# A depthwise convolution on TensorE: fp32r products with a fold, and fp32 products of 32 output columns

## The chip, the cores and the metric

The kernel runs on one core of one Trainium2 chip. Its engines are TensorE (matmul; PE in the profile, PEld its weight loads), VectorE (DVE), ScalarE (ACT), GpSimd (POOL) and SyncE (SP, which issues most DMAs). The metric is the device time of one execution in microseconds; lower is better.

## The reference, cut to what matters

A trunk of two layers handles 336 tokens (16 meta tokens, 256 prompt tokens, 8 samples of 8 tokens). Each layer mixes tokens in two ways from one projection `u = rmsnorm(h) @ w_in`: pooling windows over 512 channels, and a convolution module over 512 others. Then come a projection `w_out` and a channel mixer, dense in layer 0, eight experts in layer 1.

```python
def _conv_module(a_past, z, dw_w, dw_b, ln_g, ln_b, pw_w):      # CONV_KERNEL = 31 taps
    v = z[..., :CONV_WIDTH] * jax.nn.sigmoid(z[..., CONV_WIDTH:])
    ext = jnp.concatenate([a_past.astype(v.dtype), v], axis=1)
    y = lax.conv_general_dilated(ext, dw_w[:, None, :], window_strides=(1,), padding='VALID',
        dimension_numbers=('NWC', 'WIO', 'NWC'), feature_group_count=CONV_WIDTH) + dw_b
    y = jax.nn.silu(_layernorm(y, ln_g, ln_b))
    return y @ pw_w, ext[:, ext.shape[1] - CONV_BUF:]
```

The convolution is depthwise: each of the 512 channels has its own 31 taps. The change touches the 272 tokens of meta and prompt; the 64 sample tokens are convolved on VectorE before and after.

## The kernel before, in words

Channels lie on partitions, tokens along the free dimension; the 512 channels make four tiles, c = 0 to 3, of 128. Weights stream through a ring of six buffers (`raw`); ScalarE rounds each slot to fp32r (`w_hi`), VectorE makes the rest (`w_lo`), both in rings of three, and a product is three fp32r matmuls (`mm3`: hi·hi, hi·lo, lo·hi; lines 1747 to 1749). PSUM has six banks for products in turn: every group of products waits for the evacuation of the group six earlier (`evac`, counted in one fixed order, `GROUP`).

The projection `w_in` is worked in six slots of 256 columns in the order 2, 4, 3, 5, 1, 0 (`w_in_slot(0)` to `w_in_slot(4)`, then the last by hand): values and gates of channel tiles 0 and 1, values and gates of tiles 2 and 3, then the pooling channels. When both halves of a gate are there, VectorE forms v (`gated`, after a tanh on ScalarE) into `conv_ext`. SP then writes a tile to DRAM (`shifted`) and reads it back in another layout (`x_turned`): partition 32 i + j holds channel j of a group g of 32 channels, shifted by some tokens that depend on i. So one matmul with 128 rows takes four taps of 32 channels at once.

Before the change a tile goes this way:

1. `tap_blocks` (VectorE, L1312): stationary blocks of 128 x 128 from the taps, in a hi and a lo part, into the buffers `w_hi` and `w_lo` that the weight slots use too.
2. `turned_high` (ScalarE, L931) and `turned_low` (VectorE, L1320): hi and lo of `x_turned`, 1168 columns.
3. `conv_parts` (TensorE): for each of the four groups g, two shifts of three fp32r matmuls of 276 columns into a bank. The output partitions 32 q + j are partial sums that belong q tokens apart.
4. `part_rows` (ScalarE, L948): copies of 32 partitions and two banks, each quarter q shifted by q tokens, into `raw`; one `evac` for two banks.
5. `conv_fold` (TensorE, L1927): four fp32 matmuls with a stationary of ones (`spread_blk`) add the quarters up into one bank; `conv_with_bias` (ScalarE) moves it to `y`.

TensorE's order is `w_in_slot(2)`, half of slot 3, `conv_parts(0)`, the other half, `conv_parts(1)`, `conv_fold(0)`, `w_in_slot(4)`, `conv_fold(1)`, `conv_parts(2)`, `conv_parts(3)`, both last folds, and then the layer norm: the mean (L1906), half of the last `w_in` slot with the sums of squares inside (L1962), and the spread of the factor (L1779), after which the pointwise product can follow. VectorE's order is written out by hand as well; `conv_samples` (L1256, L1258), the tokens of the samples, fills it between the steps. GpSimd's pooling windows (L708 to L718) start with `pool_in(4, 0)` on VectorE.

Of the kernel before, what the change touches and what calls it, by code (L numbers as in the profile page):

```python
# [15 lines left out]
P = 128  # L16
MM_BANKS = 6
RAW = 6
SPLIT = 3
# [4 lines left out]
def hybrid_trunk(nc, x_prompt, x_sample, state_pool, state_conv, meta_tokens, norm1_g, w_in, pool_w,  # L24
# [35 lines left out]
    SHIFTS = 2  # L60
    NX = TP + NB
    XW = CSEG + 2
    XN = NX + NB * NB * (SHIFTS - 1)
    TAPW = NB * NB * SHIFTS
    ZERO = P - BLK
    O_COLS = NB * TP
# [39 lines left out]
    def plan_parts(l, c):  # L106
        if len(GROUP) % 2:
            plan(("even", l, c))
        plan(*[("part", l, c, g) for g in range(NB)])

    plan(*[("x", k) for k in range(KD // 2)], ("params",), *[("x", k) for k in range(KD // 2, KD)])
    for l in range(L):
# [3 lines left out]
        plan(("win", l, 2 * WIN_ORDER[3]))  # L116
        plan_parts(l, 0)
        plan(("win", l, 2 * WIN_ORDER[3] + 1))
        plan_parts(l, 1)
        plan(("conv", l, 0), *[("win", l, 2 * WIN_ORDER[4] + i) for i in (0, 1)], ("conv", l, 1))  # L120
        plan_parts(l, 2)
        plan_parts(l, 3)
        plan(("conv", l, 2), ("conv", l, 3))
# [20 lines left out]
    with ExitStack() as ctx:  # L144
# [15 lines left out]
        spread_blk = wide[:, 0:ZERO + P]  # L160
        one_blk = wide[:, ZERO:ZERO + BLK]
# [21 lines left out]
        tap_hi = sb("tap_hi", [P, L * KC, TAPW], F32R, dense)  # L183
        tap_lo = sb("tap_lo", [P, L * KC, TAPW], F32, dense)
# [9 lines left out]
        y_pool = sb("y_pool", [P, NG, T], F32, mixer)  # L194
        m_all = sb("m_all", [P, 2, KD, T], F32R, mixer)
# [7 lines left out]

        m_flat = m_all[:].rearrange("p i k t -> p (i k t)")
        turned = m_flat[:, 0:4 * NB * XN].rearrange("p (b h g n) -> p b h g n", b=2, h=2, g=NB)

# [74 lines left out]
        TAP_BLOCKS = ps[:, 7, P:P + NB * L * KC * 2 * NB].rearrange("p (g o n) -> p g o n", g=NB, o=L * KC)  # L281
# [17 lines left out]
        e_hi_done, e_lo_done, y_ready = sem("e_hi_done"), sem("e_lo_done"), sem("y_ready")  # L299
        tap_hi_done, tap_lo_done, taps_spread = sem("tap_hi_done"), sem("tap_lo_done"), sem("taps_spread")  # L300
        blocks_done, factors_done = sem("blocks_done"), sem("factors_done")
        part_out = sem("part_out")
        e_sent = [sem(f"e_sent{i}") for i in (0, 1)]
        e_turned = [sem(f"e_turned{i}") for i in (0, 1)]
# [126 lines left out]
        def parts_out(l, c):  # L431
            return tile_raw(l, c)[:, 0:O_COLS].rearrange("p (g t) -> p g t", g=NB)

# [8 lines left out]
        def dense_used():  # L442
            out, n_w = [], 0
            for n in range(MOE_BASE):
# [8 lines left out]
                elif b == FFN_BASE:  # L453
                    u, i = divmod(n - b, 2)
                    out.append((mm_done, GROUP[("gu", u, 2 * i + 1)] + 1))
                else:
                    l, i = MIX_BASE.index(b), n - b
                    last = (("win", l, 2 * WIN_ORDER[W_AT.index(i)] + 1) if i in W_AT else
                            ("part", l, D_AT.index(i), NB - 1) if i in D_AT else
                            ("pool", l, POOL_ORDER[-1]) if i == S_POOL_W else  # L460
                            ("pw", l, KC - 1) if i == S_PW else ("wout", l, 2 * (i - S_OUT) + 1))
                    out.append((mm_done, GROUP[last] + 1))
# [16 lines left out]
        def wait_used_dense(eng, n):  # L479
            s, v = DENSE_USED[n]  # L480
            eng.wait_ge(s, v)
# [55 lines left out]
        def _(sp):  # L537
# [8 lines left out]
            def turn_tiles(l, half):  # L546
# [6 lines left out]
                for c in tiles:  # L553
# [87 lines left out]
        def _(pool):  # L641
# [15 lines left out]
            link(nc.gpsimd.memset(spread_blk, 0.0))  # L657
# [205 lines left out]
        def _(act):  # L863
# [18 lines left out]
            def mixer_layer(l):  # L882
# [43 lines left out]
                def turned_high(c):  # L926

                    act.wait_ge(e_turned[c % 2], 16 * NB * (2 * l + c // 2 + 1))
                    if c > 1:
                        act.wait_ge(mm_done, GROUP[("part", l, c - 2, NB - 1)] + 1)  # L930
                    nc.scalar.activation(turned[:, c % 2, 0], x_turned(l, c), ACT.Copy).then_inc(e_hi_done, 1)  # L931

# [5 lines left out]
                def part_rows(c, pairs=(0, 2)):  # L938

                    if pairs[0] == 0 and ("even", l, c) in GROUP:  # L940
                        act.wait_ge(evac, GROUP[("even", l, c)])
                        act.sem_inc(evac, 1)
                    for g in pairs:
                        at = GROUP[("part", l, c, g)]
                        act.wait_ge(mm_done, at + 2)
                        for q in range(NB):
                            rows = slice(BLK * q, BLK * (q + 1))
                            nc.scalar.activation(parts_out(l, c)[rows, g:g + 2, :],  # L948
                                                 ps[rows, at % MM_BANKS:at % MM_BANKS + 2, q:q + TP], ACT.Copy
                                                 ).then_inc(part_out, 1)  # L950
                        act.wait_ge(part_out, 2 * NB * (KC * l + c) + NB * (g // 2 + 1))
                        act.wait_ge(evac, at)
                        act.sem_inc(evac, 2)

                past_rows()
                gated(0)
                if l == 0:
                    act.wait_ge(taps_spread, 1)
                    nc.scalar.activation(tap_hi[:].rearrange("p o (g n) -> p g o n", g=NB), TAP_BLOCKS, ACT.Copy
                                         ).then_inc(tap_hi_done, 1)  # L960
# [12 lines left out]
                part_rows(3)  # L973
                conv_with_bias(2)
# [6 lines left out]
                split_to(b + W_AT[5])  # L981
                conv_with_bias(3)
# [182 lines left out]
        def _(dve):  # L1165
# [79 lines left out]
            def mixer_layer(l):  # L1245
# [30 lines left out]
                def value(half):  # L1276
                    for i in (0, 1):
# [25 lines left out]
                def tap_blocks(c):  # L1303

                    if l == 0 and c == 0:
                        dve.wait_ge(tap_lo_done, 1)
                        dve.wait_ge(consts, 2)
                    n = b + D_AT[c]
                    _, hi, lo = parts(n, slot_size(n))
                    wait_used_dense(dve, n - SPLIT)  # L1310
                    for out, taps in ((hi, tap_hi[:, KC * l + c, :].bitcast(F32)), (lo, tap_lo[:, KC * l + c, :])):
                        nc.vector.tensor_tensor(out.rearrange("p (k n) -> p k n", k=TAPW),  # L1312
                                                one_blk.unsqueeze(1).broadcast_to([P, TAPW, BLK]),
                                                taps.unsqueeze(2).broadcast_to([P, TAPW, BLK]), ALU.mult
                                                ).then_inc(blocks_done, 1)

                def turned_low(c):

                    dve.wait_ge(e_hi_done, KC * l + c + 1)
                    nc.vector.tensor_tensor(turned[:, c % 2, 1], x_turned(l, c), turned[:, c % 2, 0].bitcast(F32),  # L1320
                                            ALU.subtract).then_inc(e_lo_done, 1)
# [15 lines left out]
                if l == 0:  # L1337
                    dve.wait_ge(tap_hi_done, 1)
                    nc.vector.tensor_tensor(tap_lo[:].rearrange("p o (g n) -> p g o n", g=NB), TAP_BLOCKS,
                                            tap_hi[:].bitcast(F32).rearrange("p o (g n) -> p g o n", g=NB), ALU.subtract  # L1340
                                            ).then_inc(tap_lo_done, 1)
# [392 lines left out]
        def _(pe):  # L1734
# [98 lines left out]
            def mixer_layer(l):  # L1833
# [56 lines left out]
                if l == 0:  # L1890

                    pe.wait_ge(consts, 2)
                    for g in range(NB):
                        for i in range(NB):
                            taps = tap_rows.rearrange("p o (m j) -> p o m j", m=SHIFTS)[:, :, :, NB * i:NB * (i + 1)]
                            ins = nc.tensor.matmul(TAP_BLOCKS[:, g].rearrange("p o (m q) -> p o m q", m=SHIFTS),
# [11 lines left out]
                def conv_parts(c):  # L1908

                    hi, lo = dense_slot(b + D_AT[c], P)  # L1910
                    pe.wait_ge(blocks_done, 2 * (KC * l + c + 1))
                    pe.wait_ge(e_lo_done, KC * l + c + 1)
                    for g in range(NB):
                        out = group(("part", l, c, g))
# [311 lines left out]
```

## Time and profile before

| | before |
|---|---|
| median of 3 runs | 1523.79 us (1523.72 to 1525.31) |
| the profiled execution | 1527.42 us |
| its span, first to last instruction | 1525.6 us |
| PE, DVE, ACT busy | 1477.9, 1203.8, 964.3 us |
| experts' stage | 547 to 1506 us of the span |

Times below are microseconds from the start of the profiled span unless marked ns. Busy time of an engine counts overlapping instructions once. A matmul of fp32 operands shows as two records, each with its weight load; one of fp32r operands as one.

### The profile page before, as it was taken

What the parts mean: (1) busy time and instruction counts of PE and PEld (TensorE: products, weight loads), DVE (VectorE), ACT (ScalarE), POOL (GpSimd) and SP (SyncE); (2) the same over time, 40 slices, a digit from 0 to 9 for tenths busy, and PEclk for the clock granted to TensorE, in tenths of its full rate; (3) what the DMA queues carried; (4) which work ended last, traced back from release to release, by engine and by line L of the source; (5) the groups of instructions that cost most, each with busy time, mean ns of one, the idle gap of its engine ahead of it and who ended that gap; (6) DMA issues with size and microseconds to landing.
All of it is one profiled execution on the core that took longest, in us unless ns stands there. A gap on an engine that the chain in (4) does not pass through costs nothing.

```text
span 1525.6 us, 20888 instructions
## 1 busy us (share of the span) xinstructions
PE 1477.9 (97%) x7639; PEld 1288.8 (84%) x7639; DVE 1203.8 (79%) x1001; ACT 964.3 (63%) x812; POOL 185.0 (12%) x216
## 2 busy tenths in 40 slices
PE   8989999999988999999999999999999999999995
PEld 7979999999987987888888888888888888888884
DVE  4887755544488578988888888888888888888888
ACT  4574334333256377777777777777777777777773
POOL 1156100002124106910000000000000000000002
PEclk9999999999998999999999999999999999999998
DMA  6455998344055569999999999999999999999994
GB/s 198 114 194 157 313 301 241 97 155 143 31 139 167 168 211 391 395 379 396 377 388 367 378 386 370 373 390 366 385 387 358 387 385 360 389 381 370 384 380 137
DMA packets 249678, 453.40 MB, mean 297 GB/s; under 512 B 9605, under 2 KB 99781, under 8 KB 249631
## 3 DMA queue, kind: packets, MB, share of 16 engines
q1 hardware_dynamic: 245056, 442.20, 81.5%
q0 software_dynamic: 2960, 9.73, 2.1%
q10 hardware_dynamic: 1615, 0.85, 0.2%
q8 instruction: 28, 0.46, 0.1%
q14 instruction: 19, 0.16, 0.0%
HBM read 426.38 MB, written 26.37 MB: 297 GB/s over the span
## 4 chain that ended last, share of the span: by engine, by line
issue 55%; PE 6%; POOL 4%; DMA 2%; DVE 1%; ACT 1%; POOLq 0%; DVEq 0%; ACTq 0%
PE ps L1747 1%; PE ps L1748 1%; PE ps L1749 1%; POOL xg L775 1%; POOL h L799 1%; DMA xg<-og,row_i 1%; DMA og<-obuf,out_row_i 0%; DMA h<-last_row 0%; DMA last_row<-last_pos 0%; POOL key L787 0%; PE ps L2104 0%; POOL pick L795 0%; POOL og L808 0%; DVE w_lo L531 0%; PE ps L2002 0%
## 5 line engine op out<-in xcount | busy, mean ns | idle before, releaser
L531 DVE TENSOR_TENSOR w_lo<-raw,w_hi 128x2048 fp32r<-128x2048 f32 x336 | 764.5, 2290 | 117.5 <-ACT w_hi L526 116.3
L526 ACT ACTIVATE w_hi<-raw 128x2048 fp32r<-128x2048 f32 x334 | 639.5, 1916 | 123.7 <-PE ps L1749 122.2
L1749 PE MATMUL ps<-w_hi,xg_lo 128*128 128x512 f32 x896 | 351.4, 392 | 0.0
L1748 PE MATMUL ps<-w_lo,xg_hi 128*128 128x512 f32 x896 | 350.8, 391 | 0.0
L1747 PE MATMUL ps<-w_hi,xg_hi 128*128 128x512 f32 x896 | 350.8, 391 | 0.0
L1748 PEld LDWEIGHTS ps<-w_lo,xg_hi 128*128 128x128 f32 x896 | 168.3, 188 | 37.2
L1747 PEld LDWEIGHTS ps<-w_hi,xg_hi 128*128 128x128 f32 x896 | 168.3, 188 | 36.8 <-DVE w_lo L531 0.2
L1749 PEld LDWEIGHTS ps<-w_hi,xg_lo 128*128 128x128 f32 x896 | 168.3, 188 | 36.0
L1747 PE MATMUL ps<-x_hi,w_hi 128*128 128x336 f32 x580 | 187.8, 324 | 8.1 <-DVE x_lo L1412 3.2
L1748 PE MATMUL ps<-x_lo,w_hi 128*128 128x336 f32 x580 | 184.9, 319 | 0.0
L1749 PE MATMUL ps<-x_hi,w_lo 128*128 128x336 f32 x580 | 184.1, 317 | 0.0
L1747 PE MATMUL ps<-w_hi,ft_hi 128*128 128x512 f32 x448 | 180.4, 403 | 0.3 <-DVE w_lo L531 0.3
L1749 PE MATMUL ps<-w_hi,ft_lo 128*128 128x512 f32 x448 | 176.0, 393 | 0.0
L1748 PE MATMUL ps<-w_lo,ft_hi 128*128 128x512 f32 x448 | 175.4, 392 | 0.0
L511 DVE TENSOR_TENSOR w_lo<-raw,w_hi 128x2048 fp32r<-128x2048 f32 (+3 forms) x39 | 80.2, 2062 | 55.5 <-ACT w_hi L502 54.1
L1747 PEld LDWEIGHTS ps<-x_hi,w_hi 128*128 128x128 f32 x580 | 110.1, 190 | 12.1 <-issue 5.7
L808 POOL DMA_INDIRECT og<-obuf,out_row_i x6 | 10.3, 1712 | 830.3 <-SPq L633 828.7
L502 ACT ACTIVATE w_hi<-raw 128x2048 fp32r<-128x2048 f32 (+3 forms) x41 | 70.3, 1721 | 63.5 <-PE ps L1749 62.2
L1748 PEld LDWEIGHTS ps<-x_lo,w_hi 128*128 128x128 f32 x580 | 110.1, 190 | 0.4
L1749 PEld LDWEIGHTS ps<-x_hi,w_lo 128*128 128x128 f32 x580 | 109.8, 189 | 0.0
L1749 PEld LDWEIGHTS ps<-w_hi,ft_lo 128*128 128x128 f32 x448 | 84.1, 188 | 18.6
L1747 PEld LDWEIGHTS ps<-w_hi,ft_hi 128*128 128x128 f32 x448 | 84.2, 188 | 17.4 <-DVE w_lo L531 1.2
(288 smaller groups left out, 1711.5 us busy)
## 6 DMA issues: line engine op xcount, KB each, us to landing
raw<-in_moe_w_gate_dram SPq DMA_DIRECT2D x112, 1024.0 KB, 7.4
raw<-in_moe_w_up_dram SPq DMA_DIRECT2D x112, 1024.0 KB, 7.6
raw<-in_moe_w_down_dram SPq DMA_DIRECT2D x112, 1024.0 KB, 7.5
raw<-in_w_in_dram SPq DMA_DIRECT2D x11, 1024.0 KB, 5.1
raw<-in_ffn_w_gate_dram SPq DMA_DIRECT2D x11, 1024.0 KB, 6.0
raw<-in_ffn_w_up_dram SPq DMA_DIRECT2D x11, 1024.0 KB, 6.3
raw<-in_w_out_dram SPq DMA_DIRECT2D x8, 1024.0 KB, 5.5
obuf<-ones SPq DMA_DIRECT2D x15, 512.0 KB, 8.0
```

The source lines that it names most:

```text
L502: nc.scalar.activation(hi, r, ACT.Copy).then_inc(hi_done, 1)
L511: nc.vector.tensor_tensor(lo, r, hi.bitcast(F32), ALU.subtract).then_inc(lo_done, 1)
L526: nc.scalar.activation(hi, r, ACT.Copy).then_inc(hi_done, 1)
L531: nc.vector.tensor_tensor(lo, r, hi.bitcast(F32), ALU.subtract).then_inc(lo_done, 1)
L775: nc.gpsimd.indirect_dma_start(out=xg, out_offset=bass.IndirectOffsetOnAxis(ap=row_i[:, t, k:k + 1], axis=0), in_=hs[:, t, :], in_offset=N ...
L799: link(nc.gpsimd.tensor_tensor(pick_e[:, i, NE * c:NE * (c + 1)], pick[:, i, NE * c:NE * (c + 1)], iota_e[:], ALU.mult))
L808: nc.gpsimd.indirect_dma_start(out=og[:, i, t, :], out_offset=None, in_=obuf, in_offset=bass.IndirectOffsetOnAxis(ap=out_row_i[:, i, t:t + ...
L1747: nc.tensor.matmul(out, a_hi, b_hi, start=start, stop=False)
L1748: nc.tensor.matmul(out, a_hi, b_lo, start=False, stop=False)
L1749: return nc.tensor.matmul(out, a_lo, b_hi, start=False, stop=stop)
```

## The change

A tile is now convolved with 32 fp32 matmuls: for each of eight steps r and each group g, a stationary of 128 rows and 32 columns, placed at columns 32 g of the array, so that its output is the partitions 32 g to 32 g + 31 of one bank. The four taps 4 r to 4 r + 3 lie in the 128 rows, and all eight steps add up in PSUM. So the fold, the copies of partial sums, `turned` and the hi and lo of taps and blocks go; the stationary blocks (`blocks`) are fp32 of their own, in memory that `m_all` takes later. `x_turned` is read back with shifts of one token and not four, 300 columns and not 292. The diag slots no longer write `w_hi` and `w_lo`, and the wait of a later split goes back to the slot before them. The order on TensorE, VectorE and ScalarE changes with it. Core of the diff:

```diff
+    STEPS = 8
-    XN = NX + NB * NB * (SHIFTS - 1)
-    TAPW = NB * NB * SHIFTS
+    XN = TP + NB * (STEPS - 1)
+    TAPW = NB * STEPS
...
+        plan(*[("win", l, 2 * WIN_ORDER[3] + i) for i in (0, 1)], ("conv", l, 0), ("conv", l, 1))
+        plan(*[("win", l, 2 * WIN_ORDER[4] + i) for i in (0, 1)], ("conv", l, 2), ("conv", l, 3))
...
+        blocks = sb("blocks", [P, KC, TAPW, BLK], F32, diag)
...
         def wait_used_dense(eng, n):
+            while n >= 0 and is_diag(n):
+                n -= SPLIT
+            if n < 0:
+                return
...
-                        src = shifted[KC * l + c].rearrange("(g c) n -> c g n", g=NB)[:, :, NB * i:NB * i + XN]
-                        sp.dma_start(x_turned(l, c)[BLK * i:BLK * (i + 1)], src).then_inc(e_turned[c % 2], 16)
+                        src = shifted[KC * l + c].rearrange("(g c) n -> c g n", g=NB)[:, :, i:i + XN]
+                        sp.dma_start(x_turned(l, c)[BLK * i:BLK * (i + 1)], src).then_inc(e_turned[c], 16)
...
         @block.scalar
...
-                turned_high(0)
-                turned_high(1)
-                part_rows(0, (0,))
                 split_to(b + W_AT[4])
-                part_rows(0, (2,))
                 gated(1)
-                part_rows(1)
                 conv_with_bias(0)
-                turned_high(2)
-                turned_high(3)
                 conv_with_bias(1)
-                part_rows(2)
-                part_rows(3)
-                conv_with_bias(2)
...
                 split_to(b + W_AT[5])
+                conv_with_bias(2)
                 conv_with_bias(3)
...
         @block.vector
...
                 split_to(b + W_AT[3])
                 tap_blocks(0)
-                value(1)
-                turned_low(0)
                 tap_blocks(1)
-                turned_low(1)
-                gate(1, (0,))
-                conv_samples(0)
-                dve.wait_ge(evac, GROUP[("part", l, 0, NB - 1)] + 1)
-                gate(1, (1,))
+                value(1, (0,))
+                conv_samples(0, (0,))
+                value(1, (1,))
+                conv_samples(0, (1,))
+                gate(1)
                 gated(1)
                 split_to(b + W_AT[4])
                 tap_blocks(2)
                 tap_blocks(3)
-                dve.wait_ge(evac, GROUP[("conv", l, 0)] + 1)
+                conv_samples(1)
+                dve.wait_ge(evac, GROUP[("conv", l, 1)] + 1)
                 pool_in(4, 0)
-                split_to(b + D_AT[3])
-                conv_samples(1, (0,))
-                turned_low(2)
-                turned_low(3)
                 pool_in(4, 1)
-                conv_samples(1, (1,))
                 conv_samples(2)
                 conv_samples(3)
...
         @block.tensor
...
+                def conv_tile(c):
+                    out = group(("conv", l, c))
+                    pe.wait_ge(blocks_done, KC * l + c + 1)
+                    pe.wait_ge(e_turned[c], 16 * NB * (l + 1))
+                    for r in range(STEPS):
+                        for g in range(NB):
+                            ins = nc.tensor.matmul(out[BLK * g:BLK * (g + 1), 0:TP], blocks[:, c, STEPS * g + r, :],
+                                                   x_turned(l, c)[:, g, NB * r:NB * r + TP], start=r == 0,
+                                                   stop=r == STEPS - 1, tile_position=(0, BLK * g))
                     ins.then_inc(mm_done, 1)
...
+                w_in_slot(3)
+                conv_tile(0)
+                conv_tile(1)
+                w_in_slot(4)
+                conv_tile(2)
+                conv_tile(3)
```

## Rows read from the trace of the kernel before

**Rows 1.** The page: the span and TensorE's share of it.

```profile
span 1525.6 us, 20888 instructions
PE 1477.9 (97%) x7639; PEld 1288.8 (84%) x7639; DVE 1203.8 (79%) x1001; ACT 964.3 (63%) x812; POOL 185.0 (12%) x216
```

**Rows 2.** Windows: stretch, length, busy time of each engine, clock, DMA share, GB/s.

```profile
52.70:97.00 44.30, 36.70 (x215) 32.44 (x214) 39.84 (x43) 31.05 (x46) 17.14 (x15) 0.96 0.50 148
...
547.00:1506.00 959.00, 957.21 (x4324) 785.26 (x4324) 841.91 (x492) 719.39 (x491) 75.35 (x59) 1.00 1.01 373
```

**Rows 3.** Timeline of PE, layer 0: start, length, instruction, [idle before <- releaser].

```profile
41.55 0.40 PE L1747 MATMUL ps<-x_hi,w_hi 128*128 128x336 f32 x1
...
52.71 0.29 PE L1747 MATMUL ps<-m_all,w_hi 128*128 128x276 f32 x1
53.09 0.28 PE L1747 MATMUL ps<-m_all,w_hi 128*128 128x276 f32 x1
...
62.69 0.40 PE L1747 MATMUL ps<-m_all,w_hi 128*128 128x276 f32 x1 [1.54 <-ACTq L953]
...
67.00 0.42 PE L1747 MATMUL ps<-x_hi,w_hi 128*128 128x336 f32 x1 [0.70 <-DVE w_lo L511]
67.57 0.31 PE L1747 MATMUL ps<-x_hi,w_hi 128*128 128x336 f32 x1
68.03 0.32 PE L1747 MATMUL ps<-x_hi,w_hi 128*128 128x336 f32 x1
...
74.50 1.99 PE L1927 MATMUL ps<-raw,wide 128*128 128x272 f32 x8
...
90.51 3.55 PE L1927 MATMUL ps<-raw,wide 128*128 128x272 f32 x8 [3.30 <-ACTq L953]
93.85 2.67 PE L1906 MATMUL ps<-y,ones 128*128 128x336 f32 x8
99.15 2.43 PE L1962 MATMUL ps<-ones,z 128*112 128x1 f32 x24
104.89 0.80 PE L1779 MATMUL ps<-scratch,ones 112*128 112x336 f32 x2
```

**Rows 4.** The same timeline in layer 1: slot 2's first record, and the spread.

```profile
414.71 0.39 PE L1747 MATMUL ps<-x_hi,w_hi 128*128 128x336 f32 x1
...
484.20 0.73 PE L1779 MATMUL ps<-scratch,ones 112*128 112x336 f32 x2
```

**Rows 5.** Lines by source: count, ns least/median/most, first and last start.

```profile
L1962 PE MATMUL ps<-ones,z x48: 165/237/237, 99.1 to 479.2; 128*112 128x1 f32 x48
L1927 PE MATMUL ps<-raw,wide x64: 390/392/793, 64.3 to 470.4; 128*128 128x272 f32 x64
L948 ACT ACTIVATE raw<-ps x64: 613/616/622, 55.3 to 466.2; 32x544 f32<-32x544 f32 x64
L1312 DVE TENSOR_TENSOR w_hi<-wide,tap_hi x8: 1217/1220/1222, 44.9 to 445.7; 128x1024 fp32r<-128x1024 f32 x8
```

**Rows 6.** Timeline of ACT, layer 0: the first use of a tile read back.

```profile
48.34 1.18 ACT L931 ACTIVATE m_all<-raw 128x1168 fp32r<-128x1168 f32 x1 [6.17 <-DMA raw<-shifted]
```

**Rows 7.** Timeline of POOL, layer 0: first and last of 12 rows, windows of two groups.

```profile
72.19 1.94 POOL L708 TENSOR_TENSOR win_sum<-pool_ext 128x470 f32<-128x470 f32 x1 [42.85 <-DVE pool_ext L1328]
...
90.26 0.31 POOL L718 TENSOR_TENSOR y_pool<-win_sum,pool_ext 128x64 f32<-128x64 f32 x1
```

**Rows 8.** Timeline of DVE, layer 0: sample taps, gate, first v, last split, last factor.

```profile
41.30 0.44 DVE L1296 SCALAR_TENSOR_TENSOR conv_ext<-z 128x272 f32<-128x272 f32 x1 [2.19 <-ACT z L923]
...
55.23 1.19 DVE L1256 TENSOR_TENSOR scratch<-conv_ext,params 128x992 f32<-128x992 f32 x1 [0.24 <-DVE z L1288]
...
62.66 0.51 DVE L1288 TENSOR_TENSOR z<-ps,rstd 128x336 f32<-128x336 f32 x1 [2.28 <-ACTq L953]
...
64.66 2.29 DVE L511 TENSOR_TENSOR w_lo<-raw,w_hi 128x2048 fp32r<-128x2048 f32 x1 [0.18 <-DVEq L508]
...
104.23 0.51 DVE L1209 TENSOR_TENSOR scratch<-ident,nt 112x336 f32<-112x336 f32 x1
```

More of the change, by code:

```diff
@@ L298, in hybrid_trunk @@
         m_hi_done = sem("m_hi_done")
-        e_hi_done, e_lo_done, y_ready = sem("e_hi_done"), sem("e_lo_done"), sem("y_ready")
-        tap_hi_done, tap_lo_done, taps_spread = sem("tap_hi_done"), sem("tap_lo_done"), sem("taps_spread")
+        y_ready = sem("y_ready")
+        tap_cols_done, taps_spread = sem("tap_cols_done"), sem("taps_spread")
         blocks_done, factors_done = sem("blocks_done"), sem("factors_done")
-        part_out = sem("part_out")
         e_sent = [sem(f"e_sent{i}") for i in (0, 1)]
-        e_turned = [sem(f"e_turned{i}") for i in (0, 1)]
+        e_turned = [sem(f"e_turned{c}") for c in range(KC)]
         ln_centred, ln_sq = sem("ln_centred"), sem("ln_sq")
@@ L458, in dense_used @@
                     last = (("win", l, 2 * WIN_ORDER[W_AT.index(i)] + 1) if i in W_AT else
-                            ("part", l, D_AT.index(i), NB - 1) if i in D_AT else
+                            ("conv", l, D_AT.index(i)) if i in D_AT else
                             ("pool", l, POOL_ORDER[-1]) if i == S_POOL_W else
@@ L924, in gated @@
                                              ).then_inc(tanh_done, 1)
[L926 to L931, printed above, removed]
                 def pooled_high(g):
@@ L936, in pooled_high @@
                     nc.scalar.activation(pooled_at(g)[0], y_pool[:, g, :], ACT.Copy).then_inc(pooled_hi, 1)
[L938 to L953, printed above, removed]
                 past_rows()
@@ L1275, in mixer_layer, with value @@
                 dve.sem_inc(sums_read, 1)
-                def value(half):
-                    for i in (0, 1):
+                def value(half, outs=(0, 1)):
+                    for i in outs:
                         g = ("win", l, 2 * WIN_ORDER[2 * half] + i)
@@ L1305, in tap_blocks @@
                     if l == 0 and c == 0:
-                        dve.wait_ge(tap_lo_done, 1)
+                        dve.wait_ge(tap_cols_done, 1)
                         dve.wait_ge(consts, 2)
[L1308 to L1321, printed above, removed]
+                    nc.vector.tensor_tensor(blocks[:, c], one_blk.unsqueeze(1).broadcast_to([P, TAPW, BLK]),
+                                            tap_cols[:, KC * l + c, :].unsqueeze(2).broadcast_to([P, TAPW, BLK]),
+                                            ALU.mult).then_inc(blocks_done, 1)
                 def pool_in(s, i):
@@ L1906, in mean_of @@
                     return nc.tensor.matmul(SUM_BANK, ones[:], y[:, c, :], start=(c == 0), stop=(c == KC - 1))
[L1908 to L1914, printed above, removed]
-                        for m in range(SHIFTS):
-                            at = NB * NB * m
-                            ins = mm3(out[:, 0:NX], hi[:, SHIFTS * g + m, :], lo[:, SHIFTS * g + m, :],
-                                      turned[:, c % 2, 0, g, at:at + NX], turned[:, c % 2, 1, g, at:at + NX],
-                                      m == 0, m == SHIFTS - 1)
-                        ins.then_inc(mm_done, 2 if g == 0 and ("even", l, c) in GROUP else 1)
@@ L1922, in conv_fold @@
-                def conv_fold(c):
-                    out = group(("conv", l, c))
-                    pe.wait_ge(evac, GROUP[("part", l, c, NB - 1)] + 1)
-                    for g in range(NB):
-                        ins = nc.tensor.matmul(out[:, 0:TP], spread_blk[:, ZERO - BLK * g:ZERO + P - BLK * g],
-                                               parts_out(l, c)[:, g, :], start=g == 0, stop=g == NB - 1)
-                    ins.then_inc(mm_done, 1)
-                w_in_slot(3, (0,))
-                conv_parts(0)
```

54 lines of the change are left out of this document (10 added, 44 removed).

## The prediction

> **What bounds the kernel now.** First I read the page: TensorE is busy for 97% of the span [rows 1]. That alone says little, so next come the windows by stage. In the experts' stage, 959 of the 1526 us, PE is busy for 957 at full clock [rows 2]. Nothing of that stage changes, and it starts only after the routing, which needs the whole mixer of layer 1. So what the mixers win or lose reaches the end undiminished: 959 us are moved and not shortened. In the mixer of layer 0 PE is busy for 36.7 of 44.3 us, DVE for 39.8, at a mean clock of 0.96 [rows 2]: a chain over several engines, not one full engine.
>
> The timeline of PE shows that chain. From the first record of `w_in_slot(2)` at 41.55 to the spread of the layer norm's factor at 104.89 [rows 3] are 63.3 us; in layer 1 the same two points stand at 414.71 and 484.20 [rows 4], 69.5 us. The idle times inside are waits for the copies of partial sums: 1.54 us before a product of `conv_parts(1)`, 3.30 before the last fold, and 0.70 for the split of slot 4, which follows on VectorE after a gate that itself waited 2.28 us for those copies [rows 3, 8]. I follow the kernel to that spread; behind it the order of work is the same before and after.
>
> **What goes.** On PE, per layer: 96 records of `conv_parts`, three in 0.38 us (52.71 to 53.09) [rows 3], so 12.2 us, and 32 records of the folds. Eight fold records last 1.99 us with 0.39 for the last one's own length [rows 3, 5]: (1.99 - 0.39)/7 = 0.229 us from one to the next, 7.3 us in all. Together 19.5 us. On ACT: 32 copies of 0.616 us, 19.7 us [rows 5], and four `turned_high` of 1.18 [rows 6], 4.7 us. On DVE: four of the eight `tap_blocks` products, 1.22 us each [rows 5], and four `turned_low`, no shorter than ACT's pass over the same tile. None of the ACT and DVE time counts by itself; it counts through the waits above.
>
> **What comes.** Four tiles a layer of 32 fp32 products; at two records each, as the fold's products have, that is 64 records a tile. Call C the time of a tile. The columns streamed are the fold's 272, so one record after another would cost 64 x 0.229 = 14.6 us. If four records at four column positions run at once, it is 64 x 0.057 = 3.65 us. No row of this trace shows a product at a column position, so these are the bounds. Between them stands the rate at which weight load and record follow each other when streaming costs nothing: the sums of squares stream one column, and 24 records take 2.43 us with 0.237 for the last [rows 3, 5], (2.43 - 0.24)/23 = 95 ns. Their weights have 112 columns, the new ones 32, so 95 ns is more likely too much than too little; a second record on the same columns pulls the other way. I take 95 ns: C = 6.1 us.
>
> **The chain after.** PE's work from slot 2 to the spread: slots 2, 3 and 4, 16 triples each at 0.46 us (67.57 to 68.03), 22.1; four tiles, 4C; the mean, 2.7; 13 of the 16 triples of the last slot that stand ahead of the spread, 6.0; the sums of squares, 2.4 [rows 3]; and 0.2 for semaphores, my estimate. That is 33.4 + 4C = 57.8 us if nothing else is late. So the spread comes at 41.55 + 57.8 = 99.4 for 104.89, 5.5 us sooner, and in layer 1 at 414.71 + 57.8 = 472.5 for 484.20, 11.7 sooner. Together 17.2 us.
>
> Is something else late? Three things must be ready. The tiles read back: the first tile's v was started at 41.30 and its use at 48.34 [rows 6, 8], about 7 us. Tiles 0 and 1 are wanted from 41.55 + 14.7 = 56.3 on, tiles 2 and 3 from 75.9; their v ends near 59.2, since gate, tanh and `gated` follow the end of slot 3 at 56.3 by about 3 us. So 68: in time. The 8 more columns of a read (300 for 292) are hidden by that slack. The eight DMAs and two writes of a half are as many as before on SP's queue, and what stands behind them, the load of the last `w_in` slot, is freed by `conv_tile(0)` at 62 and wanted after 88. The split of slot 4: ACT's half no longer waits for `conv_parts(0)`; DVE's starts after `gated` and takes 2.29 [rows 8], so 61.6, wanted at 68.5. At C = 3.65 it would be wanted at 63.6, still in time.
>
> GpSimd: its windows take from 72.19 to 90.57 [rows 7], 18.4 us, and start with `pool_in(4, 0)`. On DVE that now follows split (2.2), two `tap_blocks` (2.3) and `conv_samples(1)`, four operations of about 1.2 and a small one, 4.9 [rows 5, 8], so it ends at 59.2 + 2.2 + 2.3 + 4.9 + 0.7 = 69.3 at the earliest; with C = 6.1, half of slot 4 is there at 72.2 and it ends at 73. So the windows end at 87.7 at the earliest, at 91.3 with C = 6.1. Behind them on ACT and DVE stand a rounding of 0.5, the split of the pointwise weights, 1.9 and 2.3, two low parts, 0.9, and the factor, 2.7: 8.3 us. That gives 96.0 and 99.6. So at C = 6.1 PE's and GpSimd's chains end together, and for faster tiles GpSimd's is late next: it is a floor of 96.0 in layer 0 and, 373.2 us later as the whole stage is, 469.2 in layer 1. That is worth 8.9 + 15.0 = 23.9 us, the most that the change can bring. The fast end is paid for in clock: after 3.30 us of idle PE's records ran at twice their length (eight fold records in 3.55 us where 1.99 are usual) [rows 3]; with C = 3.65 PE idles before the squares and could lose some 3 us a layer in this way, so 18 to 24.
>
> **Sum.** The profiled execution took 1527.42 us for a span of 1525.6, and the median is 3.6 below it. The difference of 17.2 us is taken from both: 1510.2 for such an execution, and 1506.6 for the median, so I say 1507.
>
> One page of the Trainium skill prices the products at column positions. "TensorE: Matmul & The Clock Gate", Part 3, "The mechanism" says that matmuls on different tiles of the array start about 4 ns apart and run side by side. By that rule C would lie at the 3.65 us end and the median at 1500 to 1506. No row here shows it.
>
> **The rivals.**
>
> *Two at a time* (chance 0.32). Every row has PE's records start in the order of the program, and the two records of one fp32 product need the same columns: in the fold they are 229 ns apart, like any two. If the second record of a product waits for the first and holds up all behind it, then only the second of one position and the first of the next overlap, and a record costs 229/2 = 114 ns: C = 7.3 us. Then PE alone sets the end, 4.8 us a layer later than above: 17.2 - 9.6 = 7.6 us of gain, 1516. For it speaks the order; against it, that PE may hold one record in waiting for each position. The same section of the skill says that matmuls keep strict order in start and end; by that, the trace agrees in every row shown, and this rival is what it would make of fp32.
>
> *One after another* (0.17). The positions do not overlap: every record has all 128 rows, and the 229 ns of the fold stay. C = 14.6 us, 34 us a layer more than forecast: 68 - 17.2 = 51 us lost, 1575, and PE busy without a gap in both mixers. It decides from 17.2/8 = 2.15 us a tile above the forecast, so from 8.3 us a tile, 129 ns a record. For it speaks that the trace shows no two records that share a time by more than their tail; against it, that such records have never stood at different columns. The same section of the skill limits the overlap of a weight load with a running matmul to different row groups; by that rule these, all on the same rows, would go this way. No run here shows it.
>
> *The gain is hidden* (0.06). A wait that I have overlooked, for instance a tile that lands late because four of its reads now overlap other loads, holds `conv_tile(2)` to near 85. With what stands behind it the spread falls near 105: within 3 us of 1524.
>
> That leaves 0.45 for the forecast, its fast end included.
>
> **How the numbers follow.** The forecast's own range is 1500 to 1510. A change within 0.2%, 3 us, could not be told from none. With *two at a time* (1513 to 1519) and part of the hidden gain, the range is 1499 to 1523; left out are *one after another* and half of the hidden gain, 0.20. Faster by over 0.2%: 0.45 + 0.32 + 0.01 = 0.78; within: 0.04; slower: 0.17 + 0.01 = 0.18.
>
> **What would show it.** The records of `conv_tile`: the distance from the first to the last over 63 is 95 ns if I am right, 57, 114 or 229 if a rival is. `conv_tile(0)` starts near 56.3, `w_in_slot(4)` near 68.5 without idle time. The spread stands near 99.4 and, counted from the first record of slot 2 in layer 1, 57.8 us behind it. The experts' stage keeps its 959 us; if it doesn't, the step from mixer to end is wrong. The sum is wrong too if DVE reaches `pool_in(4, 0)` after 75, or if PE's clock in the mixer falls.

## Result and the profile after

The changed kernel takes 1508.75 us (median of 4 runs, 1508.25 to 1511.59), the kernel before 1524.55 beside it (4 runs, 1523.72 to 1528.96): a ratio of 0.9894, with an interval of 0.9871 to 0.9918. That is 15.8 us less, where 17.2 was forecast. The profiled execution fell from 1527.42 to 1509.17 us, and its page answers to [rows 1]:

```profile
span 1507.4 us, 21272 instructions
PE 1469.7 (97%) x7895; PEld 1271.2 (84%) x7895; DVE 1182.6 (78%) x984; ACT 915.7 (61%) x740; POOL 178.6 (12%) x216
```

TensorE's share says as little as before. The windows say more (columns as in [rows 2]): the experts' stage, then short stretches of layer 0's mixer.

```profile
528.80:1487.80 959.00, 956.32 (x4317) 784.13 (x4315) 841.98 (x493) 718.40 (x489) 75.72 (x59) 1.00 1.01 373
...
84.00:86.00 2.00, 0.26 (x1) 0.27 (x2) 1.56 (x4) 0.00 (x0) 1.72 (x4) 0.72 0.00 0
86.00:88.00 2.00, 1.85 (x4) 0.90 (x5) 2.00 (x2) 1.96 (x2) 0.00 (x0) 0.50 0.49 121
88.00:90.00 2.00, 2.00 (x8) 2.00 (x8) 2.00 (x5) 1.52 (x4) 0.00 (x0) 0.50 1.08 377
96.00:98.00 2.00, 2.00 (x9) 2.00 (x8) 1.14 (x5) 0.00 (x0) 0.00 (x0) 0.50 1.10 348
```

The first row is the 959 us of [rows 2], moved by 18.2: busy for 956.3, as before. The others are new: TensorE does almost nothing from 84 to 86, and then its granted clock is 0.50, its lower level of 1.2 GHz, and again at 96 to 98. The timeline of PE in layer 0, to be read beside [rows 3], shows what surrounds this:

```profile
43.04 0.41 PE L1678 MATMUL ps<-x_hi,w_hi 128*128 128x336 f32 x1
...
57.99 7.54 PE L1846 MATMUL ps<-raw,blocks 128*32 128x272 f32 x128
65.46 0.42 PE L1678 MATMUL ps<-x_hi,w_hi 128*128 128x336 f32 x1
...
73.05 7.54 PE L1846 MATMUL ps<-raw,blocks 128*32 128x272 f32 x128
80.52 1.96 PE L1837 MATMUL ps<-y,ones 128*128 128x336 f32 x6
85.74 1.49 PE L1837 MATMUL ps<-y,ones 128*128 128x336 f32 x2 [3.26 <-DVEq L1214]
87.37 0.62 PE L1678 MATMUL ps<-x_hi,w_hi 128*128 128x336 f32 x1
...
92.18 2.43 PE L1876 MATMUL ps<-ones,z 128*112 128x1 f32 x24
94.47 0.40 PE L1678 MATMUL ps<-x_hi,w_hi 128*128 128x336 f32 x1
...
99.33 0.45 PE L1710 MATMUL ps<-scratch,ones 112*128 112x336 f32 x1
```

Two tiles are one row: 128 records in 7.54 us. The length of one record stands in the view of the line:

```profile
L1846 PEld LDWEIGHTS ps<-raw,blocks x512: 106/110/110, 58.0 to 444.7; 128*32 128x32 f32 x171
L1846 PE MATMUL ps<-raw,blocks x512: 392/392/417, 58.0 to 444.9; 128*32 128x272 f32 x171
```

So a record costs (7.54 - 0.39)/127 = 56.3 ns on average, and a tile takes 64 x 0.0563 = 3.6 us. A record still lasts 392 ns in the profile, as in the fold; 229/4 = 57 is what four at a time would give, and it is what they do. Windows of 0.03 us on this line (PE's busy time and records touched, the same for weight loads, clock, DMA share, GB/s) show the four:

```profile
59.09:59.12 0.03, 0.03 (x8) 0.00 (x0) 1.00 0.00 0
59.12:59.15 0.03, 0.03 (x4) 0.00 (x0) 1.00 0.00 0
59.15:59.18 0.03, 0.03 (x7) 0.01 (x3) 1.00 0.00 0
59.18:59.21 0.03, 0.03 (x8) 0.03 (x4) 1.00 0.00 0
```

Four old records run on while four new ones start within about 0.03 us, and four weight loads run beside them. Slot 4 starts at 65.46 without a wait. The chain from slot 2 to the spread is 99.33 - 43.04 = 56.3 us, where it was 63.3. Layer 1 repeats it, 464.62 - 407.77 = 56.85 for 69.5 [rows 4]:

```profile
407.77 0.40 PE L1678 MATMUL ps<-x_hi,w_hi 128*128 128x336 f32 x1
...
451.08 1.49 PE L1837 MATMUL ps<-y,ones 128*128 128x336 f32 x2 [3.87 <-DVEq L1214]
...
464.62 0.73 PE L1710 MATMUL ps<-scratch,ones 112*128 112x336 f32 x2
```

The two chains are 7.05 and 12.64 us shorter, 19.7 together. The span is 18.2 shorter: slot 2 of layer 0 began 1.5 us later, at 43.04 for 41.55. That is not the change's doing: the spread of the first norm, ahead of everything changed, starts anywhere from 35.5 to 38.3 us in the thirteen profiled kernels of this study. Between the two chains the changed kernel is 1.4 us quicker (308.44 for 309.82 us) and behind layer 1's spread 1.4 us slower (1042.8 for 1041.4); the two cancel, and their cause stays open.

What keeps TensorE waiting stands in the timelines of the other engines, layer 0 (compare [rows 7, 8]):

```profile
73.15 0.44 DVE L1268 TENSOR_TENSOR pool_ext<-ps,rstd 128x272 f32<-128x272 f32 x1 [2.51 <-PE ps L1680]
73.77 1.18 DVE L1209 TENSOR_TENSOR scratch<-conv_ext,params 128x992 f32<-128x992 f32 x1
...
82.26 1.83 DVE L1209 TENSOR_TENSOR scratch<-conv_ext,params 128x992 f32<-128x992 f32 x1
84.12 1.19 DVE L1211 TENSOR_REDUCE y<-scratch 128x32 f32<-128x992 f32 x1
85.35 0.28 DVE L1213 TENSOR_SCALAR y<-y,params 128x64 f32<-128x64 f32 x1
```

```profile
70.73 0.96 POOL L694 TENSOR_TENSOR win_sum<-pool_ext 128x470 f32<-128x470 f32 x1 [40.02 <-DVE pool_ext L1270]
...
85.65 0.31 POOL L704 TENSOR_TENSOR y_pool<-win_sum,pool_ext 128x64 f32<-128x64 f32 x1
```

```profile
86.04 0.48 ACT L915 ACTIVATE m_all<-y_pool 128x336 fp32r<-128x336 f32 x1 [3.71 <-POOLq L707]
86.43 1.90 ACT L488 ACTIVATE w_hi<-raw 128x2048 fp32r<-128x2048 f32 x1
88.81 1.73 ACT L942 ACTIVATE z<-y 128x336 f32<-128x336 f32 x4 [0.48 <-DVE y L1326]
```

Two chains end together. VectorE's sums for the sample rows of tiles 2 and 3 (`conv_samples`, 73.77 to 85.63) hold up the mean's last product. GpSimd's windows (to 85.96) hold up ScalarE's rounding, and with it the split and the squares queued behind. The first shows on PE, the second is hidden behind it by half a microsecond. The first goes on after 85.63: VectorE's low part of the pooling weights (`w_lo`, L1318) stands behind the sums, and slot 5 on PE needs it. In layer 0 of e8, the same kernel again, the mean's last product ran at the upper clock, and slot 5 waited for that split:

```profile
85.75 0.83 PE L1837 MATMUL ps<-y,ones 128*128 128x336 f32 x2 [3.27 <-DVEq L1214]
87.38 0.40 PE L1678 MATMUL ps<-x_hi,w_hi 128*128 128x336 f32 x1 [0.80 <-DVE w_lo L1318]
```

It started at 87.38, as at 87.37 above.

### The profile page after: what moved, and what is told of

Same layout as the page of the kernel before. It is cut to its first block, busy times and chain, and to the rows that moved or that the text cites. A ratio compares the mean times of both kernels' runs of the same rounds, so it can differ in the third digit from the quotient of the medians.

```text
span 1507.4 us, 21272 instructions
## 1 busy us (share of the span) xinstructions
PE 1469.7 (97%) x7895; PEld 1271.2 (84%) x7895; DVE 1182.6 (78%) x984; ACT 915.7 (61%) x740; POOL 178.6 (12%) x216
## 4 chain that ended last, share of the span: by engine, by line
PE 67%; DVE 1%; ACT 1%; issue 1%; DVEq 0%; ACTq 0%
PE ps L1680 21%; PE ps L1678 21%; PE ps L1679 21%; PE ps L2039 2%; ACT w_hi L512 0%; PE ps L2029 0%; PE ps L2018 0%; DVE w_lo L517 0%; PE ps L1916 0%; PE ps L1761 0%; DVE yt L1660 0%; PE ps L1946 0%; PE ps L2107 0%; DVE act_f L1581 0%; PE ps L1876 0%
```

## The experiments

Each kernel is the changed one with the edit that is shown. Each ratio is against the kernel before, measured beside it: 1525.87 us for e1 to e4, 1524.41 for e5 to e8, 1525.82 for e9 to e11. The last columns are, for each layer, the time from the spread of the norm ahead of the mixer to the spread of the layer norm's factor, from the timeline of PE; the stretch holds all that was changed and leaves out the drift of the start.

| kernel | median us | ratio (interval) | layer 0 | layer 1 |
|---|---|---|---|---|
| before | 1524.55 | 1 | 69.3 | 72.0 |
| changed | 1508.75 | 0.9894 (0.9871 to 0.9918) | 62.4 | 59.3 |
| e8, changed, again | 1508.51 | 0.9888 (0.9869 to 0.9908) | 62.0 | 59.3 |
| e1, one position after another | 1556.68 | 1.0199 (1.0182 to 1.0216) | 87.4 | 82.4 |
| e2, two positions in turn | 1513.13 | 0.9910 (0.9893 to 0.9926) | 64.4 | 61.6 |
| e3, no late sample sums (a part of the result is left out) | 1501.69 | 0.9843 (0.9827 to 0.9860) | 59.0 | 56.1 |
| e4, PE kept busy | 1501.11 | 0.9835 (0.9818 to 0.9851) | 60.4 | 56.6 |
| e5, VectorE's order | 1510.79 | 0.9901 (0.9876 to 0.9926) | 60.2 | 61.2 |
| e6, ScalarE's order | 1507.79 | 0.9885 (0.9865 to 0.9906) | 62.6 | 59.4 |
| e7, both orders | 1501.68 | 0.9843 (0.9824 to 0.9862) | 59.8 | 55.8 |
| e9, both, 8 and 8 products | 1502.51 | 0.9853 (0.9834 to 0.9872) | 57.9 | 54.6 |
| e10, e4 and ScalarE's order | 1501.70 | 0.9846 (0.9828 to 0.9863) | 59.2 | 56.2 |
| e11, both, 4 and 4 products | 1499.43 | 0.9836 (0.9815 to 0.9858) | 57.0 | 54.6 |

**e1 and e2: is it the overlap of column positions?** The same 64 records a tile in another order.

```diff
-                    for r in range(STEPS):
-                        for g in range(NB):
+                    for g in range(NB):
+                        for r in range(STEPS):
```

> The changed kernel with the 32 products of a tile in another order: all eight steps of one column position, then the next position. Same products, same result. Theory (overlap by position): in the changed kernel a record follows the one before it by 56 ns because neighbours in the program stand at different column positions; with neighbours at one position it is the fold's 229 ns, 64 x 0.229 = 14.6 us a tile. PE's chain from slot 2 to the spread is then 33.4 + 4 x 14.6 = 91.8 us a layer for 56.3 and 56.9 now, 70 us more: about 1579 us. Rival (narrow weights): a record of 32 columns costs 56 ns wherever it stands; 1509 us, no change.

e2 goes over positions 0 and 1 in turn, and then over 2 and 3:

```diff
-                    for r in range(STEPS):
-                        for g in range(NB):
+                    for r, g in [(r, 2 * pair + i) for pair in (0, 1) for r in range(STEPS) for i in (0, 1)]:
```

> The changed kernel with positions 0 and 1 in turn for all eight steps, then positions 2 and 3. Theory (overlap by position, as many as stand next to each other): 229/2 = 114 ns a record, 7.3 us a tile; PE's chain is 33.4 + 29.2 = 62.6 us a layer, about 6 more than now, PE without idle time at full clock: 1517 to 1521 us, still faster than the kernel before although PE's own work for a tile (7.3 us) is more than that of the kernel before (4.9 us). Rival (a queue for each position lets all four overlap in any order): 56 ns, 1509 us. Rival (any repeat of a position drains the array): nearer to 229 ns, over 1560 us.

The tiles' rows on PE's timeline in layer 0, e1 and then e2:

```profile
58.76 23.31 PE L1846 MATMUL ps<-raw,blocks 128*32 128x272 f32 x128
```

```profile
58.90 12.22 PE L1846 MATMUL ps<-raw,blocks 128*32 128x272 f32 x128
```

(23.31 - 0.39)/127 = 180 ns a record for e1, (12.22 - 0.39)/127 = 93 ns for e2. So the gain comes from the overlap: without most of it the kernel is 31 us slower than before. Both are faster than the 229 and 114 expected, and so are the kernels (1557 for 1579, 1513 for 1517 to 1521). Windows of 0.23 us on this line show why for e1 (columns as above):

```profile
60.00:60.23 0.23, 0.23 (x3) 0.11 (x2) 1.00 0.00 0
...
62.00:62.23 0.23, 0.23 (x5) 0.14 (x2) 1.00 0.25 71
```

Inside a position three records of 0.39 us touch a window, what a step of 229 ns gives; near 62, where one position gives way to the next, five do. If records started strictly in the order of the program, 229 ns apart inside a position, a position of 16 records would take at least 15 x 0.229 = 3.4 us; 16 x 0.180 = 2.9 were measured. So records of the next position run beside the last ones of the old, and a record that waits does not block those behind it. This is worked out from the counts, since the rows don't name the position. It is the opposite of what the rival *two at a time* supposed.

e2 is by chance the tile that the forecast assumed: 64 x 0.093 = 6.0 us where 6.1 was taken. Its kernel came out at 1513, not 1507, with a chain in layer 1 of 59.1 us (410.76 to 469.88), where 33.4 + 4 x 6.0 gives 57.2. The formula holds within 2 us a layer. It also shows that the gain isn't work saved on TensorE: before, a tile's records took 3 us of parts and 1.8 of fold, less than these 6.0, and e2 is still 0.9% faster. What went are the waits for copies and the low clock behind them. The change also gave VectorE and ScalarE a new order of work; no run has the new products in the old order, so how much of the gain the order alone brings is not shown.

**e3: what is late next?**

```diff
-                conv_samples(2)
-                conv_samples(3)
+                for c in (2, 3):
+                    link(nc.vector.memset(y[:, c, TP:T], 0.0))
+                    dve.sem_inc(y_ready, 1)
```

> The changed kernel without the convolution of the sample tokens of channel tiles 2 and 3 on VectorE (those tokens are set to zero, a part of the computation that is left out). Theory (VectorE is late next): the layer norm's mean waits for these sums, PE idles over 3 us and its clock falls; without them the mean follows the last tile at once, GpSimd's windows end sooner too, the spread comes near 91 for 99.3 in layer 0, and as much in layer 1: about 1493 us. Rival (GpSimd's windows are late next, and what VectorE does beside them does not matter): the squares still start near 88.8, and only the clock is won: 1502 to 1506 us. Rival (the tiles' products are what counts): 1508 us.

Without VectorE's late sums the mixers are 3.4 and 3.3 us shorter, and the kernel is at 1501.7, not 1493. GpSimd's chain is late next, as the first rival said, though not in its way: the windows end at 82.73 for 85.96 and the squares start at 85.00, not near 88.8. The clock isn't won either; it falls behind the squares' wait, and their 24 sums take 3.35 us for 2.43. ScalarE and then PE in layer 0:

```profile
82.81 0.48 ACT L915 ACTIVATE m_all<-y_pool 128x336 fp32r<-128x336 f32 x1 [1.97 <-POOLq L707]
```

```profile
85.62 3.35 PE L1877 MATMUL ps<-ones,z 128*112 128x1 f32 x24 [1.29 <-ACT z L942]
```

**e4: is it the idle time itself, or the clock behind it?** 15 products whose result nothing reads stand ahead of the mean's last product.

```diff
                 for c in range(KC):
+                    if c == KC - 1:
+                        keep_busy(15)
                     ins = mean_of(c)
```

> The changed kernel with 15 fp32 products of 128 columns on operands that lie there anyway, ahead of the mean's last product, where PE idles 3.3 and 3.9 us. Same result. Theory (the clock is lost there): the granted clock stays at 1.00 through the last slot; the last mean product, and 13 triples of which nearly all ran at 0.84 us where 0.46 is the full speed, win some 3.5 us a layer: about 1502 us. Rival (VectorE's and ScalarE's chain to the factor sets the spread whatever PE's clock is): within 1 us of 1508.7.

```profile
83.64 3.51 PE L1715 MATMUL ps<-ones,ident 128*128 128x128 f32 x30
87.07 0.83 PE L1837 MATMUL ps<-y,ones 128*128 128x336 f32 x2
88.70 0.39 PE L1678 MATMUL ps<-x_hi,w_hi 128*128 128x336 f32 x1 [0.80 <-DVE w_lo L1318]
...
91.54 2.43 PE L1878 MATMUL ps<-ones,z 128*112 128x1 f32 x24
```

With 3.51 us of useless work the kernel is 7 us faster than the changed one. The wait is the same, filled instead of idle; but the 18 records from 88.70 to 91.54 now take 2.84 us, where they took 4.81 (87.37 to 92.18). Here the clock alone is the difference. It still falls once behind the squares' sums, at 94.1.

The mixers account for 2.0 and 2.7 us of this, 4.7 together, less than the 3.5 a layer expected. Another 3.7 came behind layer 1's spread, where nothing was edited: from there to the end of the span are 1039.0 us in e4 and in e10, 1042.8 in the changed kernel, and 1041.1 to 1043.4 in all others. (Against this, e4's first spread came 1.3 us later.) The windows about 50 us behind the spread, in the changed kernel and in e4:

```profile
514.62:516.62 2.00, 2.00 (x12) 1.68 (x11) 1.86 (x10) 1.82 (x4) 0.00 (x0) 0.59 0.95 355
516.62:518.62 2.00, 2.00 (x11) 2.00 (x12) 1.89 (x7) 1.71 (x7) 0.00 (x0) 0.50 0.07 29
```

```profile
511.26:513.26 2.00, 1.73 (x16) 1.49 (x15) 1.86 (x11) 1.83 (x4) 0.00 (x0) 1.00 1.00 375
513.26:515.26 2.00, 2.00 (x20) 1.93 (x20) 1.93 (x8) 2.00 (x8) 0.00 (x0) 1.00 0.11 38
```

The clock falls there in the changed kernel and not in e4. That the products ahead of the mean do this some 60 us later is not shown, so only the 4.7 us are theirs.

**e5, e6, e7: two chains or one?** e5 moves VectorE's sums for tiles 1 and 2 into waits that its timeline shows (between the gate's columns, and between the two `pool_in`). e6 is ScalarE alone: the split and the squares ahead of the rounding of the second group's windows, and that group's low part on VectorE behind the factor. e7 does both.

```diff
-                gate(1)
+                gate(1, (0,))
+                conv_samples(1, (0,))
+                gate(1, (1,))
...
-                conv_samples(1)
+                conv_samples(1, (1,))
...
                 pool_in(4, 0)
+                conv_samples(2, (0,))
                 pool_in(4, 1)
-                conv_samples(2)
+                conv_samples(2, (1,))
```

```diff
-                pooled_high(POOL_ORDER[1])
                 split_to(b + S_PW)
                 for c in range(KC):
                     act.wait_ge(ln_centred, KC * l + c + 1)
                     nc.scalar.activation(z[:, c, :], y[:, c, :], ACT.Square).then_inc(ln_sq, 1)
+                pooled_high(POOL_ORDER[1])
```

> The changed kernel with two half sets of sample sums moved on VectorE into its gaps: half of tile 1 ahead of the gate's second column (3.1 us idle there), half of tile 2 between the two first pooling inputs (2.5 us idle). Same result. Theory (two chains of like length stand behind each other's: VectorE's sample sums to the mean, and GpSimd's windows through ScalarE's in-order queue to the squares): the last sample sum ends 3 us sooner, PE idles less and keeps more of its clock, but ScalarE still waits for the windows ahead of the last split and the squares: 1503 to 1506 us. Rival (sample sums alone are late): 5 to 7 us a layer, 1495 to 1498.

> The changed kernel with the rounding of the second pooling group, which waits for GpSimd's windows, put behind the last split and the squares on ScalarE, and its low part behind the factor on VectorE. Same result. Theory of two chains: the squares still wait for the mean, which waits for the sample sums, so the squares move by less than 1 us and PE's clock falls as before: within 1.5 us of the changed kernel on this chip. Rival (the windows alone are late): some 3 us a layer, 6 us.

> Both reorderings together, VectorE's sample sums into its gaps and ScalarE's squares ahead of the wait for the windows. Same result. Theory of two chains: each alone wins little and both together win more than the sum, since only then neither end is late: the mean follows the tiles almost at once, PE does not idle, the spread comes about 50 us behind slot 2's first record for 56.3 and 56.9: 12 to 14 us under the changed kernel, about 1495. Rival (the gains add): the sum of the two runs above.

> The changed kernel as it is, on the same chip as the three above, as their base: 1507 to 1512 us.

Against e8, the changed kernel measured beside them, e5 gained nothing (+2.3 us, where 1503 to 1506 was expected) and e6 nothing that can be told (-0.7), but both together 6.8. That is the sign of two chains of nearly one length: either alone is covered by the other. For e5 this is so of the sum only: layer 0 is 1.7 us shorter than in e8, layer 1 1.9 longer, where PE waits 2.44 us for the squares and its clock is at the lower level from there to the spread. For e5 the row is ScalarE's:

```profile
87.95 0.48 ACT L915 ACTIVATE m_all<-y_pool 128x336 fp32r<-128x336 f32 x1 [4.83 <-POOLq L707]
```

VectorE is done sooner (84.13 for 85.63), but ScalarE's wait for GpSimd grows from 3.71 to 4.83. GpSimd's two groups of windows took 16.8 us here (71.11 to 87.87), 15.2 in the changed kernel (70.73 to 85.96) and 13.5 in e3 (69.24 to 82.73), where fewer of VectorE's sums run beside them. VectorE's product took 1.19 us at 64.57 in the changed kernel, ahead of the windows, and 1.83 at 82.26, beside them; its reductions took 1.19 in both places. So side by side both engines took longer, and moving work of the one under the other isn't free. For the windows, e3 shows it by taking the sums away; for VectorE's product no run takes the windows away.

e7 should have brought 13.5 and brought half. In its windows of layer 0 the clock is what is left:

```profile
86.00:88.00 2.00, 2.00 (x9) 2.00 (x9) 2.00 (x5) 0.82 (x2) 1.57 (x2) 0.50 1.07 375
...
94.00:96.00 2.00, 2.00 (x9) 2.00 (x9) 1.49 (x6) 0.00 (x0) 0.00 (x0) 0.50 1.10 347
```

**e9, e10, e11: both orders with TensorE kept busy.** In e7 PE idles for only 0.99 us ahead of the mean's last product and 0.88 ahead of slot 5. e9 puts 8 products at each place, e11 4; e10 is e4 with ScalarE's order.

```diff
+                    if c == KC - 1:
+                        keep_busy(4)
                     ins = mean_of(c)
                 ins.then_inc(sums_done, 1)
...
+                keep_busy(4)
                 n = b + W_AT[5]
```

> Both reorderings of the run before last (the sample sums of tiles 1 and 2 in VectorE's gaps, ScalarE's split and squares ahead of the second group's windows), and 8 plain fp32 products ahead of the mean's last product and 8 ahead of slot 5, each 8 by 0.234 us (30 records took 3.51 us) = 1.87 us. TensorE idled 0.97 and 0.88 us at these places without them. Theory that idleness ahead of slot 5 lowers the clock, and the clock eats the rest of the reorderings' gain: the clock stays at its upper level, giving back about 3.4 us in the first layer and 1.7 in the second, less 0.9 to 1.0 us a place by which the cover is longer than the gap, 3.8 in all: about 1500. Rival, the clock falls after the squares' sums whatever stands ahead of slot 5: 1503 to 1505.

> The 15 products ahead of the mean's last product, and ScalarE's order alone: split and squares ahead of the second group's windows. Theory: with the products TensorE already has no idle stretch there, so the squares are not late and their earlier start has nothing to win: 1500 to 1501.5, as with the products alone (1501.1). Rival, the squares still set the second layer's end through the factor on VectorE (0.58 us of wait there): 1499 to 1500.

> As the run with 8 and 8, but 4 and 4 products of 0.234 us, 0.94 us a place, about as long as the idle stretches of 0.97 and 0.88 us that they replace. Theory of the clock: it stays at its upper level and the cover costs nothing: 1501.7 - 3.4 - 1.7 = about 1496.5. Rival, products of 128 columns at these places do not hold the clock: 1501 to 1502.

The windows of e11, where e7's showed 0.50:

```profile
86.00:88.00 2.00, 2.00 (x16) 2.00 (x15) 2.00 (x5) 1.09 (x3) 1.30 (x2) 1.00 1.07 371
...
94.00:96.00 2.00, 1.84 (x11) 1.59 (x11) 1.97 (x7) 0.36 (x1) 0.78 (x1) 1.00 1.10 347
```

The clock stays at its upper level in both mixers, in e9 too. That 4 products of 0.23 us at a place are enough to hold it is not shown: in e7 the clock fell at these places in layer 0, but in layer 1, with gaps of 1.03 and 1.46 us, it fell only behind the squares' sums. And the mean clock of a whole execution was 0.988 in two of e11's four and 0.991 and 0.992 in the others, where e7 had 0.987 to 0.988. The mixers are 2.7 and 1.2 us shorter than e7's, 3.9 of the 5.1 expected. Of that the median shows 2.3 (1499.43, runs from 1497.8 to 1502.5), and the intervals of e4, e7, e9, e10 and e11 overlap: these versions beat both kernels by measure, but no order among them is shown. e9, with more cover than gap, should have paid 3.8 us for it; its mixers are only 0.9 us longer than e11's, 112.5 for 111.6. e10 came out as its theory said: with TensorE kept busy, the squares' earlier start wins nothing that can be told in the median. The medians of e4 and e10 hold 2 to 4 us from behind the mixers as well; by the mixers alone, both layers together, e11 takes 111.6 us, e9 112.5, e7 and e10 115.5, e4 117.0.

## Why the prediction was right, and which terms were off

**What bounds the kernel** held. The experts' stage moved and kept its length, and the gain of the two chains reached the end but for the 1.5 us of drift ahead of layer 0's slot 2, and the two differences of 1.4 us behind the chains that cancel.

**What goes** held: the waits of [rows 3] for partial sums and for slot 4's split are gone, and e2 shows that those waits, with the low clock behind them, were the larger part of the gain, rather than the 19.5 us of records.

**C, the time of a tile, was mis-sized**: 6.1 us taken from the rate of one-column records (95 ns), 3.6 measured (56.3 ns), the lower bound that the text gave. The Trainium skill's rule that was cited there ("TensorE: Matmul & The Clock Gate", Part 3, "The mechanism": tiles of the array run side by side) agrees with this row. Its condition for the overlap of a weight load, which made *one after another* a rival, differs from what these rows show: all these weights have the same 128 rows, and 512 loads of 106 to 110 ns go with records that cost 56.3 ns each, so loads do run beside records and beside one another. For the choice between bounds the nearest row was the wrong guide: the one-column records go through one position, so they could not show what four of them do.

**The floor took back nearly all of that.** Four tiles at 3.6 instead of 6.1 us should shorten a layer by another 10 us, and the chain from slot 2 by PE's work alone would be 33.4 + 14.4 = 47.8 us. It is 56.3 in layer 0. Of the 8.5 us between, 3.26 are the idle time at 85.74. Another 3.7 are the 13 triples of slot 5: 4.81 + 4.86 us where 13 x 0.46 = 6.0 is their length at the upper clock. About 1.0 stands between the mean's last product and slot 5, 1.63 us where a quarter of 2.7 is usual; e8 shows that it is the wait for VectorE's split, and not the low clock of that product. The last 0.5 are the tiles: two of them take 7.47 us to the next start, not 7.2. So the forecast's branch for fast tiles, 18 to 24 us with a loss by the clock, is what came: 19.7. In that branch one thing was overlooked. The forecast let GpSimd's windows alone be late next and didn't follow `conv_samples(2)` and `(3)` behind `pool_in(4, 1)`: 73.77 to 85.63, 11.9 us, with products that took longer beside GpSimd's windows. They, and the split behind them, are what PE waits for, not the squares; e7 shows that both chains had to be shortened. The windows themselves took 15.2 us where 18.4 was assumed, and ended at 85.96, not 87.7.

That 1507 was so near is thus in part luck: a tile 2.5 us too long stood in for a wait and a lower clock of about the same size.

**The rivals.** *Two at a time* falls by 56.3 against 114 ns, and its mechanism by e1's counts, as far as they go. *One after another* is what e1 makes on purpose: 1557 rather than 1575, since positions overlap where they meet. *The gain is hidden* didn't come: `conv_tile(2)` started at 73.05 without a wait.

**The signs.** `pool_in(4, 0)` was reached at 69.94, close to the 69.3 and well before 75. The clock in the mixer did fall, the sign that was named for a wrong sum, and e4 gives back 4.7 us of its price in the two mixers.

## What to carry to other kernels

Products of 32 output columns at four positions ran four at a time as long as successive records went to different positions; order the loop so that the position changes fastest, since the other order cost 48 us here. When a step on the critical engine becomes much shorter, list everything that must be ready at its new end, on each engine, not only the one that is late now: here two chains ended within half a microsecond of each other, and a new order for either alone brought nothing to the whole kernel. And look at the granted clock behind each new idle stretch: filling it with products that nobody reads shortened the two mixers by 4.7 us, where a new order for both chains shortened them by 6.2. Where a median moves, look in the trace for the place: in e4 nearly half of what was won came from a stretch that the edit doesn't touch.

## What the runs showed of the hardware

- fp32 records of 128 rows by 32 columns with 272 streamed columns last 392 ns each in the profile; on average one comes every 56 ns over four positions in turn (four at once, every 225 ns), 93 over two, 180 when a position is finished before the next. The last two are shorter than 229/2 and 229.
- The clock fell after 3.26 us of idle TensorE, and also in layer 0 of e5 and e7, where it idled for only about 0.97 and 0.88 us with 0.8 us of work between. It did not fall there in e4, e9, e10 and e11, whose largest gap in layer 0 at that place was 0.80, nor in layer 1 of e7, with gaps of 1.03 and 1.46.
- Behind the 24 one-column records of the squares' sums the clock fell in layer 0 of the changed kernel, e4, e5 and e7, but not of e10, whose TensorE work around that place is e4's. In e1 it fell in layer 0 and not in layer 1, in e2 the other way round. What decides that stays open.
- With VectorE and GpSimd at work together both took longer: a VectorE product of 128 x 992 up to 1.83 us for 1.19, its reductions not (1.19), the windows 16.8 us for 13.5.
